# Delta rule: the eight z products of a slot that needs new weights, from rounds 0 and 6 to 12 to rounds 6 to 12

## The chip, the cores and the metric

The kernel runs on one core of one Trainium2 chip. The metric is the device time of one execution in microseconds, and a lower one is better. All data is float32.

## The reference, cut to what matters

The program computes two transformer blocks over 256 tokens and 256 context tokens. The change lies in the delta-rule mixer of the second block. Cut to that:

```
z = proj[..., DN_CONV_W:DN_CONV_W + DN_VAL_W]          # 512 rows of tokens x 2048
def step(S, inp):
    qc, kc, vc, gc, bc = inp
    a = eye + where(strict, kk * decay * bc, 0)
    sol = triangular_solve(a, rhs)
    u, w = sol[..., :dv], sol[..., dv:]
    v_new = u - w @ S
    o = (qc * exp(gc)) @ S + qk @ v_new
    S = S * exp(g_last) + (kc * exp(g_last - gc)).T @ v_new
    return S, o
...
o = rmsnorm_2(o_f + flip(o_b), norm_g) * silu(z)
return o @ w_out
```

So z is a plain matrix product (the layer's input by 2048 columns of `dn_w_in`) which nothing in the recurrence needs: it is wanted only after it. The recurrence is a chain. Each chunk needs the inverse of a triangular matrix, and each state needs the one before.

## The kernel before, in words

The kernel is written by hand for five engines. Each engine has a program of its own (`pe_program`, `dve_program` and so on), and each runs its instructions strictly in the order written. A wait for a semaphore therefore holds all that stands behind it on that engine.

The delta rule works in **slots**, k from 0 to 17 (`pe_chunks` and its likes). A slot has 13 **rounds**, 0 to 12. In each round every engine issues, one after the other, what several generators have for that round. On TensorE these are, in this order:

- `pe_inverse` of chunk group k: a chain of four levels, each of three steps. In rounds 0, 3, 6 and 9 it transposes W (L2135), in rounds 1, 4, 7 and 10 it multiplies by N (L2143), in rounds 2, 5, 8 and 11 by T (L2151). Between the three steps VectorE makes R (L2165), ScalarE makes T (L211), and VectorE updates W (L2169).
- `pe_prep` of the next group (L2007, L2008 and L2015).
- `pe_zstep`: one 128x512 tile of z, as eight products that add up in one PSUM bank (L2454). The table `Z` says how many of the eight are issued in which round. Sixteen tiles fill slots 0 to 15. The four slots of a column chunk c = k // 4 share one weight chunk of 2 MB; i = k % 4 is the row tile.
- `pe_recur` of group k - 2: for both directions the state's products (L2281 or L2288, L2297, L199, L2318). From round 1 on, VectorE answers with the carry (L2335, four instructions a direction), ScalarE with copies and scalings (L211), GpSimd with masks.

The weights of z come through a ring of four slots. Three of them are lent out to hold other data during the delta rule, so one slot is left. `ring.use` makes TensorE wait for the load (semaphore `ring3`), and `sp_zsteps` on SyncE issues the load of the next chunk (L183) only when the last product of the chunk before (`nz.p` of slot 4c - 1, round 12) is done. On SyncE the load stands behind the z store (L2490) and two small loads of decays for the queries (L1962), and ahead of two more (L1954). ScalarE copies the finished tile in round 12.

PSUM banks are handed out by `Banks.take` from a queue of idle ones: the one that was given back first is taken first, and TensorE waits for what has to have read it. The z tile holds its bank from its first product to the end of the slot.

Of the kernel before, what the change touches and what calls it, by code (L numbers as in the profile page):

```python
# [188 lines left out]
def bc(ap, axis, n):  # L189
    u = ap.unsqueeze(axis)  # L190
    shape = list(u.shape)
    shape[axis] = n
    return u.to_broadcast(shape)
# [70 lines left out]
class Kernel:  # L264
# [1734 lines left out]
    def pe_prep(self, p, m, k):  # L1999
        P, V = self.P, self.V  # L2000
        g, c = divmod(k, 4)
        for r in range(self.ROUNDS):
# [9 lines left out]
            if r == 8:  # L2012
                p.wait_ge(*V.of("in.Z", k))
                b = self.banks.take(p, "in.ab", k)
# [67 lines left out]
    def dve_block(self, v, m, k, part):  # L2082
# [10 lines left out]
        if part == 2:  # L2093
            for d in range(2):
                t = v().tensor_tensor(m["prod"][:, 256 * d:256 * d + 256].rearrange("p (h j r) -> p h j r", h=4, j=8),
                                      bc(m["AC"][:, d], 2, 8), bc(bc(m["start"][:, 4 * d, :], 1, 4), 3, 8), ALU.mult)
                t.then_inc(*(V.up("in.Z", k) if d else V.up("in.Z0")))

# [343 lines left out]

    Z = {0: 1, 6: 1, 8: 1, 9: 2, 10: 1, 11: 1, 12: 1}

    def pe_zstep(self, p, m, k):
        c, i = divmod(k, 4)
        if i == 0:
            m["zch"] = self.ring.use(p, 8, 512)  # L2450
        b, q = self.banks.take(p, "nz.p", k), 0
        for r in range(self.ROUNDS):
            for _ in range(self.Z.get(r, 0)):
                t = p.e.matmul(b, self.hT[:, q, 128 * i:128 * i + 128], m["zch"][:, q, :], start=(q == 0), stop=(q == 7))  # L2454
                if q == 7:
                    t.then_inc(*self.P.up("nz.p", k))
                q += 1
            yield
        self.banks.give(("nz.p", k), self.A.of("nz.z", k))
        if i == 3:  # L2460
            self.ring.done(self.P.of("nz.p", k))
            if c < 3:
                m["lent"] = [self.ring.lend() for _ in range(3)]
# [1555 lines left out]
```

## Time and profile before

| | us |
|---|---|
| median of 3 runs | 4279.09 |
| lowest and highest | 4276.19, 4282.1 |
| span of the profiled execution | 4275.4 |
| TensorE busy | 3506.1 (82%) |
| VectorE busy | 2659.6 (62%) |
| ScalarE busy | 1401.6 (33%) |
| GpSimd busy | 1205.5 (28%) |
| mean granted TensorE clock (1 is 2.4 GHz) | 0.947 |

The profile was taken from one execution. Of its own time only the span, from the first to the last instruction, is shown. It is 3.7 us below the median of the runs. Slots 0 to 15 of the delta rule lie between about 1262 and 1847 us of the span. The wait of an instruction is shown behind it in square brackets, with what ended it. A float32 matmul is recorded as two instructions, so one product of z is an entry "x2".

### The profile page before, as it was taken

What the parts mean: (1) busy time and instruction counts of PE and PEld (TensorE: products, weight loads), DVE (VectorE), ACT (ScalarE), POOL (GpSimd) and SP (SyncE); (2) the same over time, 40 slices, a digit from 0 to 9 for tenths busy, and PEclk for the clock granted to TensorE, in tenths of its full rate; (3) what the DMA queues carried; (4) which work ended last, traced back from release to release, by engine and by line L of the source; (5) the groups of instructions that cost most, each with busy time, mean ns of one, the idle gap of its engine ahead of it and who ended that gap; (6) DMA issues with size and microseconds to landing.
All of it is one profiled execution on the core that took longest, in us unless ns stands there. A gap on an engine that the chain in (4) does not pass through costs nothing.

```text
span 4275.4 us, 38801 instructions
## 1 busy us (share of the span) xinstructions
PE 3506.1 (82%) x11382; PEld 1852.2 (43%) x11382; DVE 2659.6 (62%) x5456; ACT 1401.6 (33%) x3747; POOL 1205.5 (28%) x1228
## 2 busy tenths in 40 slices
PE   7888978999867677779998987877788787877877
PEld 3334436844335555567554542322233256322222
DVE  3656455849656666633779658777555455887444
ACT  1232120004524544441333333433433221433333
POOL 0001100001005444520333433433434201434432
PEclk9889989999989998989999999999999998999999
DMA  5523324645321111043899999999999723999998
GB/s 215 197 79 136 121 85 165 224 165 189 138 71 33 52 52 57 17 166 143 349 415 397 406 409 421 403 422 421 409 417 413 326 79 142 413 421 414 417 421 360
DMA packets 169764, 1088.28 MB, mean 255 GB/s; under 512 B 16432, under 2 KB 45488, under 8 KB 51152
## 3 DMA queue, kind: packets, MB, share of 16 engines
q0 software_dynamic: 112608, 820.04, 46.7%
q1 hardware_dynamic: 56944, 265.77, 16.9%
q8 instruction: 90, 1.47, 0.1%
q14 instruction: 122, 1.00, 0.1%
HBM read 1075.19 MB, written 10.55 MB: 254 GB/s over the span
## 4 chain that ended last, share of the span: by engine, by line
PE 34%; DVE 24%; DMA 18%; issue 12%; POOL 7%; ACT 6%; DVEq 0%; SPq 0%; POOLq 0%; ACTq 0%
PE bank L199 19%; DMA arena<-in_uv,arena 15%; POOL arena L3018 6%; DVE arena L3035 6%; ACT arena L211 5%; PE bank L2986 4%; DVE arena L443 2%; PE bank L1620 2%; DVE arena L561 2%; PE bank L2454 2%; DVE arena L217 1%; PE bank L2151 1%; PE bank L2143 1%; DVE arena L221 1%; DMA arena<-in_w_rows 1%
## 5 line engine op out<-in xcount | busy, mean ns | idle before, releaser
L2986 PE MATMUL bank<-arena 128*128 128x512 f32 x3072 | 1486.8, 618 | 355.0 <-ACT arena L211 352.2
L211 ACT ACTIVATE arena<-arena 128x1 f32<-128x1 f32 (+4 forms) x2831 | 949.6, 335 | 2005.7 <-DVE arena L3035 1123.7
L199 PE MATMUL bank<-arena 128*128 128x256 f32 (+4 forms) x4640 | 1298.6, 439 | 69.8 <-ACT arena L211 35.3
L3035 DVE CUSTOM_DVE_ANT_0 arena<-arena 128x1024 f32<-128x1024 f32 x768 | 941.8, 1226 | 607.2 <-DMA arena<-in_uv,arena 568.9
L3018 POOL DMA_INDIRECT arena<-in_uv,arena x768 | 791.0, 1030 | 1254.2 <-PE bank L2986 856.7
L2986 PEld LDWEIGHTS bank<-arena 128*128 128x128 f32 x3072 | 544.5, 191 | 1269.9 <-ACT arena L211 825.4
L199 PEld LDWEIGHTS bank<-arena 128*128 128x128 f32 (+2 forms) x4640 | 805.1, 196 | 551.9 <-issue 424.2
L211 ACT ACTIVATE arena<-bank 128x512 f32<-128x512 f32 (+4 forms) x306 | 160.8, 525 | 496.5 <-PE bank L199 318.6
L443 DVE CUSTOM_DVE_ANT_0 arena<-arena 128x1024 f32<-128x1024 f32 x192 | 241.2, 1256 | 33.5 <-DMA arena<-in_w_rows 21.9
L211 ACT ACTIVATE arena<-bank,arena 128x128 f32<-128x128 f32 (+1 forms) x400 | 162.4, 406 | 286.8 <-PE bank L2143 224.2
L626 POOL TENSOR_SCALAR arena<-arena 128x1 f32<-128x1 f32 (+3 forms) x48 | 16.2, 337 | 665.2 <-ACT arena L211 471.0
L561 DVE SCALAR_TENSOR_TENSOR arena<-bank,arena 128x508 f32<-128x508 f32 (+2 forms) x248 | 159.0, 641 | 8.8
L2454 PE MATMUL bank<-arena 128*128 128x512 f32 x256 | 134.3, 628 | 30.3 <-DMA arena<-in_dn_w 30.3
L211 ACT ACT_TABLE_LOAD x92 | 118.0, 1283 | 79.4 <-DMA arena<-gates_rest 26.5
L217 DVE TENSOR_SCALAR arena<-bank,arena 128x256 f32<-128x256 f32 (+3 forms) x162 | 84.1, 519 | 88.4 <-PE bank L520 48.4
L2151 PE MATMUL bank<-arena 128*128 128x128 f32 x512 | 75.7, 292 | 60.5 <-ACT arena L211 60.5
L2201 POOL TENSOR_TENSOR arena<-arena 128x512 f32<-128x512 f32 x64 | 81.2, 1269 | 117.0 <-DVE arena L2169 70.0
L2194 POOL TENSOR_TENSOR arena<-arena 128x512 f32<-128x512 f32 x64 | 82.5, 1290 | 99.6 <-PE bank L2143 96.4
L216 DVE TENSOR_SCALAR arena<-bank,arena 128x256 f32<-128x256 f32 (+5 forms) x98 | 55.4, 565 | 80.6 <-PE bank L199 63.1
L2151 PEld LDWEIGHTS bank<-arena 128*128 128x128 f32 x512 | 63.2, 194 | 86.3 <-ACT arena L211 85.7
L2169 DVE TENSOR_TENSOR arena<-arena,bank 128x512 f32<-128x512 f32 x64 | 44.0, 687 | 75.9 <-PE bank L2151 73.5
L221 DVE TENSOR_REDUCE arena<-arena 128x32 f32<-128x512 f32 (+10 forms) x99 | 66.1, 668 | 39.9 <-ACT arena L211 34.4
(251 smaller groups left out, 2493.4 us busy)
## 6 DMA issues: line engine op xcount, KB each, us to landing
arena<-in_w_rows SPq DMA_DIRECT2D x50, 1024.0 KB, 5.0
arena<-in_w_in SPq DMA_DIRECT2D x16, 2048.0 KB, 8.0
arena<-in_wq SPq DMA_DIRECT2D x14, 2048.0 KB, 8.5
arena<-in_dn_w SPq DMA_DIRECT2D x12, 2048.0 KB, 10.0
arena<-in_w_up SPq DMA_DIRECT2D x11, 2048.0 KB, 7.9
arena<-in_dn_wo SPq DMA_DIRECT2D x8, 2048.0 KB, 11.3
arena<-in_w_rows POOLq DMA_DIRECT2D x14, 1024.0 KB, 5.7
arena<-decay_rest SPq DMA_DIRECT2D x56, 256.0 KB, 5.0
```

Source lines behind the costliest of these rows:

```text
L199: t = p.e.matmul(out, l, r, start=(i == 0), stop=(i == n - 1))
L211: return a().activation(out, in_, f, **kw)
L217: return v().tensor_scalar(out, a, s1, s2, op0, op1)
L221: return v().tensor_reduce(out, a, AX, op)
L443: v().tensor_tensor_reduce(trash, w[:, j, :], self.crow[r], 1.0, 0.0, ALU.mult, ALU.add, self.M[m][:, j0 + j, c:c + 1]).then_inc(*(V.up("m ...
L561: t = v().scalar_tensor_tensor(dst[:, :, o], src[:, :, f], wc(d + h), dst[:, :, o], ALU.mult, ALU.add)
L1620: t = p.e.matmul(bs[n], m["act"][:, 4 * c + k, 128 * i:128 * i + 128], ch[:, k, 512 * half:512 * half + 512], start=(c + k == 0), stop=(4 ...
L2151: t = p.e.matmul(b[:, H4[h]], m["T"][:, H4[h]], m["B"][:, H4[h]], start=True, stop=True)
L2454: t = p.e.matmul(b, self.hT[:, q, 128 * i:128 * i + 128], m["zch"][:, q, :], start=(q == 0), stop=(q == 7))
L2986: t = p.e.matmul(by[half], m["dg"][ee % 4], m["uv"][r][:, 1024 + 512 * half:1536 + 512 * half], start=(ee == 0), stop=(ee == 127))
L3018: g.e.indirect_dma_start(out=m["uv"][q % 7], out_offset=None, in_=self.I["uv"], in_offset=bass.IndirectOffsetOnAxis(ap=m["idx"][n % 2][:, ...
L3035: v().tensor_tensor_reduce(self.spare, uv[:, 0:1024], m["ht"][n % 2], 1.0, 0.0, ALU.mult, ALU.add, m["acts"][:, ee:ee + 1]).then_inc(*V.up ...
```

## The change

`Z` becomes two tables. A slot with i = 0 (slots 0, 4, 8 and 12, where a new weight chunk is needed) issues its eight products in rounds 6, 7, 8, 9 (two), 10, 11 and 12. The other slots keep round 0 and rounds 6, 8, 9 (two), 10, 11 and 12. `ring.use` and `banks.take` are called right ahead of the first product and no longer at the slot's start.

```
-    Z = {0: 1, 6: 1, 8: 1, 9: 2, 10: 1, 11: 1, 12: 1}
+    Z = ({6: 1, 7: 1, 8: 1, 9: 2, 10: 1, 11: 1, 12: 1}, {0: 1, 6: 1, 8: 1, 9: 2, 10: 1, 11: 1, 12: 1})
...
         c, i = divmod(k, 4)
-        if i == 0:
-            m["zch"] = self.ring.use(p, 8, 512)
-        b, q = self.banks.take(p, "nz.p", k), 0
+        q = 0
         for r in range(self.ROUNDS):
-            for _ in range(self.Z.get(r, 0)):
+            for _ in range(self.Z[min(i, 1)].get(r, 0)):
+                if q == 0:
+                    if i == 0:
+                        m["zch"] = self.ring.use(p, 8, 512)
+                    b = self.banks.take(p, "nz.p", k)
                 t = p.e.matmul(b, self.hT[:, q, 128 * i:128 * i + 128], m["zch"][:, q, :], start=(q == 0), stop=(q == 7))
```

The order of the other engines' and of SyncE's instructions stays. On TensorE, the start of slot 4 before (the last product of slot 3, the transposes of round 0, then the z product with the wait for the weights, then round 0 to 3 of the others):

```order
L2454 MATMUL bank<-arena 128x512 x2
L2135 MATMUL bank<-arena 128x128 x4
L2454 MATMUL bank<-arena 128x512
L2288 MATMUL bank<-arena 128x256 x2
L2143 MATMUL bank<-arena 128x128 x4
L2288 MATMUL bank<-arena 128x256 x2
L2151 MATMUL bank<-arena 128x128 x4
L2297 MATMUL bank<-arena 128x128 x4
L2135 MATMUL bank<-arena 128x128 x4
```

The same place in the changed program (lines below the diff are two higher, so z is L2456):

```order
L2456 MATMUL bank<-arena 128x512 x2
L2135 MATMUL bank<-arena 128x128 x4
L2288 MATMUL bank<-arena 128x256 x2
L2143 MATMUL bank<-arena 128x128 x4
L2288 MATMUL bank<-arena 128x256 x2
L2151 MATMUL bank<-arena 128x128 x4
L2297 MATMUL bank<-arena 128x128 x4
L2135 MATMUL bank<-arena 128x128 x4
```

The z product of round 0 is gone, and with it the wait that stood ahead of L2288, L2143 and all the rest of the slot.

On TensorE, rounds 6 to 8 of slot 4 before:

```order
L2135 MATMUL bank<-arena 128x128 x4
L2454 MATMUL bank<-arena 128x512
L2318 MATMUL bank<-arena 128x256 x2
L2143 MATMUL bank<-arena 128x128 x4
L2318 MATMUL bank<-arena 128x256 x2
L2151 MATMUL bank<-arena 128x128 x4
```

And in the changed program:

```order
L2135 MATMUL bank<-arena 128x128 x4
L2456 MATMUL bank<-arena 128x512
L2318 MATMUL bank<-arena 128x256 x2
L2143 MATMUL bank<-arena 128x128 x4
L2456 MATMUL bank<-arena 128x512
L2318 MATMUL bank<-arena 128x256 x2
L2151 MATMUL bank<-arena 128x128 x4
```

The product of round 6 is now the slot's first and carries the wait for the weights; a second one stands in round 7, between L2143 and the second L2318.

## Rows read from the trace of the kernel before

**Rows 1.** The page, part 1: busy time of each engine, share of the span.

```profile
PE 3506.1 (82%) x11382; PEld 1852.2 (43%) x11382; DVE 2659.6 (62%) x5456; ACT 1401.6 (33%) x3747; POOL 1205.5 (28%) x1228
```

**Rows 2.** Waits: who waited for whom, us in total, times, longest.

```profile
PE bank L2454 <- DMA arena<-in_dn_w: 30.3, 3, 10.3
```

**Rows 3.** Timeline of TensorE, slot 4 to round 3: start, us, instruction, idle before.

```profile
1396.62 0.66 PE L2135 MATMUL bank<-arena 128*128 128x128 f32 x4 [1.91 <-DVE arena L2121]
1407.56 2.08 PE L2454 MATMUL bank<-arena 128*128 128x512 f32 x2 [10.29 <-DMA arena<-in_dn_w]
1409.43 1.91 PE L2288 MATMUL bank<-arena 128*128 128x256 f32 x4
...
1416.95 0.66 PE L2135 MATMUL bank<-arena 128*128 128x128 f32 x4 [0.68 <-DVE arena L2169]
```

**Rows 4.** Busy time in stretches: PE, PEld, DVE, ACT, POOL, granted clock, DMA.

```profile
1396.00:1400.00 4.00, 0.66 (x4) 0.42 (x4) 1.25 (x2) 2.68 (x7) 2.54 (x3) 0.78 0.48 137
1400.00:1407.00 7.00, 0.00 (x0) 0.00 (x0) 0.00 (x0) 0.00 (x0) 0.00 (x0) 0.50 1.00 385
```

**Rows 5.** Timeline of TensorE, slot 5 from round 0 to round 3.

```profile
1443.10 0.66 PE L2135 MATMUL bank<-arena 128*128 128x128 f32 x4 [1.90 <-DVE arena L2121]
...
1444.46 1.03 PE L2288 MATMUL bank<-arena 128*128 128x256 f32 x4
1445.32 1.05 PE L2143 MATMUL bank<-arena 128*128 128x128 f32 x8
...
1448.03 1.16 PE L2151 MATMUL bank<-arena 128*128 128x128 f32 x8 [0.79 <-ACT arena L211]
...
1450.77 0.66 PE L2135 MATMUL bank<-arena 128*128 128x128 f32 x4 [0.68 <-DVE arena L2169]
```

**Rows 6.** Timeline of VectorE, slot 5, the same rounds.

```profile
1445.52 1.51 DVE L2335 SCALAR_TENSOR_TENSOR arena<-bank,arena 128x128 f32<-128x128 f32 x4 [1.03 <-PE bank L2288]
...
1448.41 1.51 DVE L2335 SCALAR_TENSOR_TENSOR arena<-bank,arena 128x128 f32<-128x128 f32 x4
1450.02 0.69 DVE L2169 TENSOR_TENSOR arena<-arena,bank 128x512 f32<-128x512 f32 x1
```

**Rows 7.** Timeline of TensorE, slot 5, rounds 6 and 7: a product that waits for R.

```profile
1459.85 0.60 PE L2135 MATMUL bank<-arena 128*128 128x128 f32 x4
...
1461.68 1.13 PE L2143 MATMUL bank<-arena 128*128 128x128 f32 x8 [0.37 <-DVE arena L2165]
```

**Rows 8.** Timeline of TensorE, round 0 and round 3 of slot 8, then of slot 12.

```profile
1546.02 0.66 PE L2135 MATMUL bank<-arena 128*128 128x128 f32 x4 [1.91 <-DVE arena L2121]
...
1565.69 0.66 PE L2135 MATMUL bank<-arena 128*128 128x128 f32 x4
...
1698.36 0.91 PE L2135 MATMUL bank<-arena 128*128 128x128 f32 x4 [1.91 <-DVE arena L2121]
...
1718.05 0.66 PE L2135 MATMUL bank<-arena 128*128 128x128 f32 x4 [0.68 <-DVE arena L2169]
```

**Rows 9.** Timeline of TensorE, slot 4, z of round 6 and L2151 of round 8.

```profile
1425.17 1.02 PE L2454 MATMUL bank<-arena 128*128 128x512 f32 x2
...
1430.75 1.16 PE L2151 MATMUL bank<-arena 128*128 128x128 f32 x8 [1.94 <-ACT arena L211]
```

**Rows 10.** Timeline of SyncE: the issue of slot 4's weights.

```profile
1396.83 0.50 SPq L183 DMA_DIRECT2D arena<-in_dn_w  x1
```

**Rows 11.** DMA issues from 1396.8 to 1397.5 us: KB, us to landing.

```profile
arena<-in_dn_w SPq DMA_DIRECT2D x1, 2048.0 KB, 10.7
```

**Rows 12.** Landing of the eight L183 loads issued from 1243 to 1886 us.

```profile
DMA to landing us min/median/max: 10.3/11.6/30.1
```

**Rows 13.** Landing of the two query decays (L1962) issued at 1395.7 and 1396.2.

```profile
DMA to landing us min/median/max: 6.0/6.2/6.3
```

**Rows 14.** Timeline of TensorE, round 0 and round 3 of slot 11.

```profile
1663.99 0.67 PE L2135 MATMUL bank<-arena 128*128 128x128 f32 x4 [2.07 <-DVE arena L2121]
...
1673.34 0.66 PE L2135 MATMUL bank<-arena 128*128 128x128 f32 x4 [0.68 <-DVE arena L2169]
```

## The prediction

> **What bounds the kernel now.** I read the busy shares first, then the waits, then the timelines of the engines around the slots that need new weights.
>
> TensorE is busy 82% of the span and no other engine over 62% [rows 1]. A share says little about one stage, so the question is what TensorE waits for in the delta rule. The list of waits has one row that the change can touch. The z product (L2454) waited three times for its weights, 30.3 us in all and 10.3 at most [rows 2]. It is three and not four because slot 0's weights are loaded long before; slots 4, 8 and 12 wait.
>
> The timeline shows what that wait holds up. In slot 4 TensorE issues the transposes of round 0 at 1396.62. The z product behind them starts at 1407.56, after 10.29 us of nothing [rows 3]. The load was issued at 1396.83 [rows 10] and took 10.7 us [rows 11], so it landed at 1407.5. During this, from 1400 to 1407, no engine does anything at all, and the clock of TensorE stands at 0.50, its 1.2 GHz level [rows 4]. The reader should see that everybody's next step needs a TensorE product that is queued behind z. The wait is thus bare in full. Its end is cold as well: L2288 takes 1.91 us behind it [rows 3] against 1.03 in slot 5 [rows 5].
>
> From the transposes of round 0 to those of round 3, a slot with this wait takes 1416.95 - 1396.62 = 20.33 us in slot 4 [rows 3], 19.67 in slot 8 and 19.69 in slot 12 [rows 8]. Slot 5 does the same work, its z product of round 0 included, in 1450.77 - 1443.10 = 7.67 us [rows 5].
>
> **The change, part by part.**
>
> *The wait leaves round 0.* Compared with slot 5, slots 4, 8 and 12 lose 12.66, 12.00 and 12.02 us: 36.7 in all. This is 30.3 of bare wait and 6.4 of cold clock behind it.
>
> *The z product leaves round 0.* In slot 5 L2288 starts 1.36 us after the transposes and L2143 2.22 after them [rows 5]. Between them and the transposes stands one z product, 0.86 from start to start, as from L2288 to L2143. Which chain does it lengthen? On VectorE the first carry starts at 1445.52, 1.06 after L2288; the second carry starts 2.89 later, takes 1.51 and is followed by the update of W at 1450.02 and by the transposes at 1450.77 [rows 5, 6]. Without z, this chain starts 0.86 earlier: round 3 would come 7.67 - 0.86 = 6.81 after round 0. The other chain goes through R. Where TensorE waits for R it starts L2143 1.83 after the transposes [rows 7], so L2143 moves from 2.22 to 1.83 and not by the full 0.86. L2151 follows 2.71 after L2143 and lasts 1.16 [rows 5]: it ends at 1.83 + 2.71 + 1.16 = 5.70. The second carry ends at (1448.41 - 1443.10) - 0.86 + 1.51 = 5.96. The carry is later, and its 6.81 stands. Bounds: 0 and 0.86 per slot; I take 0.86, since this chain ends last in the rows.
>
> So the three slots save 20.33 - 6.81 = 13.52, 19.67 - 6.81 = 12.86 and 19.69 - 6.81 = 12.88: 39.3 us. Slot 0 has no wait and no carry, only the R chain: I credit 0.4 (2.22 - 1.83), bounds 0 and 0.86.
>
> *A z product comes to round 7.* It stands between L2143 and the second L2318, and the next thing on TensorE, L2151, waits 1.94 us for ScalarE in slot 4 [rows 9]. The product needs 0.86 of that. The second L2318 comes 0.86 later, and VectorE's and ScalarE's answers to it are needed only in later rounds. Cost: nothing, as long as ScalarE ends last there. If that cover is gone, it is 0.86 in each of four slots, 3.4 us. I take 0.
>
> *The wait moves to round 6.* Behind it on TensorE would stand both L2318, L2143 of round 7 and all the rest, and every engine behind those. Is it still a wait? Before, z of round 6 started at 1425.17 [rows 9], 28.55 after the transposes of round 0. Shortened by 13.52 it comes at 15.03. The load is issued 0.21 after these transposes and takes 10.7 [rows 10, 11]: it lands at 10.9. The margin is 4.1 us in slot 4. So I take 0. The nearest row is that very load; the far bound is the longest landing among the eight big loads of this half, 30.1 us [rows 12], and it makes a rival.
>
> *SyncE and its queue.* The load's place in SyncE's order and its release (the last z product of the slot before) do not change, nor does any DMA. But what was hidden under the wait may now be late. The query decays issued ahead of the load land 6.0 to 6.3 us after their issue [rows 13], so by about 1402.5. ScalarE needs the first of them in round 2, whose L2151 would begin at 1396.62 + 1.83 + 2.71 = 1401.2, behind another exponential. So this is tight: between 0 and 1402.5 - 1401.2 = 1.3 a slot. I take 0, since that exponential waits for VectorE's work behind the first carry.
>
> *The bank.* The z tile takes its bank six rounds later. Banks are reused in the order in which they came back. So before round 6 one bank more is idle and every wait for a bank gets slack; from round 6 on the queue is as before. Cost 0.
>
> *The clock.* TensorE falls to 1.2 GHz at some slot starts even without a wait for weights. Slot 11 needs 1673.34 - 1663.99 = 9.35 us to round 3 [rows 14], 1.68 more than slot 5. I charge one of the three slots with that: -1.7 of gain. Bounds: none of them, or all three and slot 0 (6.7).
>
> **Sum:** 39.3 + 0.4 - 1.7 = 38.0 us. All of it is on the path, since all engines stand still in the wait and the stages behind the delta rule start on its last instruction. Against the profiled execution, 4275.4 - 38.0 = 4237.4 of span. The median of the runs is 3.7 above that span, so I forecast 4279.1 - 38.0 = **4241.1 us**.
>
> **The rivals.**
>
> *Cold starts.* With no product between the transposes and L2288, TensorE does less at the start of a slot, where it has just idled for 1.91 us. If that drops the clock in all four slots, the gain is 39.7 - 4 x 1.68 = 33.0, time 4246. For it: slot 11 fell with z in place. Against: slot 5 stayed at full speed after the same idle time, and 0.86 us of work is little. The Trainium skill ("TensorE: Matmul & The Clock Gate", "What's actually happening") says that the low clock is the default and that activity lifts it. By that rule the wait costs more than its length, as the trace shows with 0.50; but by the same rule a product used as filler at a sparse place is worth something, and the change takes it away. The sum by it would be this rival's.
>
> *Backlog.* The wait let the others catch up. From 1396 to 1400 ScalarE worked 2.68 us and GpSimd 2.54 [rows 4]. If this work now delays the slot, each gives back up to 2.7: gain 38.0 - 8.1 = 29.9, time 4249. Against: slot 5 starts with the same work on both and needs 7.67.
>
> *The load is late in round 6.* If it lands more than 4.1 us later because four engines now work beside it, each microsecond more costs one per slot. At 18 us instead of 10.7 it is 3 x 3.2 = 9.6 of wait: gain 28, time 4251, or less gain with a cold clock behind it. Against: the DMA traffic is the same as before.
>
> *Nothing arrives.* The time comes back at a later stage: 4279. I see no stage that starts on anything but the delta rule's end.
>
> *Slower: the load becomes as slow as the slowest of its kind.* At 30.1 us [rows 12] it lands 30.3 after the transposes. TensorE then waits 15.3 us in round 6, and z of round 6 comes at 30.3 instead of 28.55: 1.8 later than before. The clock is down again behind it, some 2.2 us (6.4 / 3). That is 4 per slot, 12 in all: 4291. It decides from a landing of about 26 us on. Against: the 30.1 belongs to a burst of several 2 MB loads; here there is one such load beside four small ones.
>
> **How the numbers follow.** Forecast 0.68, cold starts 0.12, backlog 0.08, late load 0.05, nothing 0.03, slower 0.04. About 0.2% (8.6 us) is what a measurement of this kernel can tell from no change. The first four cases are all faster than that: 0.93; same 0.03; slower 0.04. The range goes from 4234 (no clock charge, 39.7, and the runs' own spread of 3 us and a little more) to 4252 (backlog, or the late load).
>
> **What would show it.** Right: no wait for in_dn_w on L2456; the other engines busy between round 0 and round 3 of slots 4, 8 and 12; 6.8 us for that stretch; the idle time ahead of L2151 in round 8 down from 1.94 to about 1.1; the delta rule shorter by 38, everything behind it as long as before. Wrong: a wait for weights at round 6 (late load); more than 8 us for the stretch at full clock (backlog) or at 1.2 GHz (cold starts); an unchanged end with a new wait behind the delta rule.

## The result and the profile after

The changed kernel takes 4234.72 us (median of 4 runs, 4233.56 to 4238.67), the kernel before 4280.6 (4 runs, 4276.19 to 4282.99). The ratio is 0.9896, with a 95% interval from 0.9883 to 0.9909. The gain is 45.9 us, against 38.0 forecast; the time forecast was 4241.1, and 4234.72 lies only 0.7 us above the lower end of the stated range (4234 to 4252). Between the two profiled executions the span fell from 4275.4 to 4231.8, by 43.6.

Page, part 1, of the changed kernel: the instructions of each engine are as many as in [rows 1], and their busy times differ by 16 us at most, while the span is 43.6 shorter.

```profile
span 4231.8 us, 38794 instructions
PE 3498.2 (83%) x11382; PEld 1848.0 (44%) x11382; DVE 2659.4 (63%) x5456; ACT 1401.4 (33%) x3747; POOL 1221.3 (29%) x1228
```

What the z product (now L2456) waited for, and who waited for it, from the view of its line. The row of [rows 2] has no counterpart: nothing in this list is a DMA.

```profile
its engine sat idle before it (us, times) until:
  issue: 22.9, 94
who waited for it (us, times):
  ACT arena L211: 42.3, 16
```

Timeline of TensorE in slot 4, from round 0 to round 3 and then rounds 6 to 8. It answers to [rows 3, 9].

```profile
1397.58 0.66 PE L2135 MATMUL bank<-arena 128*128 128x128 f32 x4 [1.91 <-DVE arena L2121]
1398.07 1.03 PE L2288 MATMUL bank<-arena 128*128 128x256 f32 x4
1399.11 1.13 PE L2143 MATMUL bank<-arena 128*128 128x128 f32 x8
...
1404.74 0.66 PE L2135 MATMUL bank<-arena 128*128 128x128 f32 x4 [0.79 <-DVE arena L2169]
...
1412.95 1.02 PE L2456 MATMUL bank<-arena 128*128 128x512 f32 x2
...
1415.57 1.02 PE L2456 MATMUL bank<-arena 128*128 128x512 f32 x2
...
1418.53 1.16 PE L2151 MATMUL bank<-arena 128*128 128x128 f32 x8 [1.07 <-ACT arena L211]
1419.52 1.02 PE L2015 MATMUL bank<-arena 128*128 128x512 f32 x2
```

Round 0 to round 3 takes 1404.74 - 1397.58 = 7.16 us where it took 20.33. The first z product starts 15.37 us after the transposes, the second fills part of the idle time ahead of L2151, which is 1.07 in place of 1.94.

The load is issued at the same place, and the same stretches as in [rows 4] now hold work of every engine at full clock (columns: stretch, length, PE, PEld, DVE, ACT, POOL, granted clock, DMA share, GB/s). The weights still arrive after 10.7 us beside it (365 GB/s from 1400 to 1407, against 385).

```profile
1397.80 0.50 SPq L183 DMA_DIRECT2D arena<-in_dn_w  x1
```

```profile
arena<-in_dn_w SPq DMA_DIRECT2D x1, 2048.0 KB, 10.7
```

```profile
1396.00:1400.00 4.00, 2.41 (x16) 1.99 (x17) 2.87 (x9) 3.52 (x9) 2.36 (x4) 1.00 0.36 109
1400.00:1407.00 7.00, 5.42 (x43) 4.77 (x42) 5.63 (x10) 5.43 (x12) 3.65 (x4) 1.00 0.98 365
```

To see where the time went, I took the start of the round-0 transposes of every slot from the TensorE timelines of both kernels, and the first matmul behind the last z product of slot 15 (1847.51 and 1807.89) as the end.

| us | before | after | gain |
|---|---|---|---|
| start of slot 0 | 1268.28 | 1266.97 | 1.3 |
| slot 0 | 31.86 | 34.35 | -2.5 |
| slot 4 (to round 3) | 46.48 (20.33) | 33.29 (7.16) | 13.2 |
| slot 8 | 45.87 (19.67) | 33.34 (7.16) | 12.5 |
| slot 12 | 47.58 (19.69) | 33.86 (7.68) | 13.7 |
| the other twelve slots together | 407.44 | 406.08 | 1.4 |
| all of slots 0 to 15 | 579.23 | 540.92 | 38.3 |
| from there to the end of the span | 2427.9 | 2423.9 | 4.0 |

So the gain sits where it was looked for. Of the 39.4 us of slots 4, 8 and 12, 37.7 lie ahead of round 3. The other 1.7 lie in round 8 of slot 12: there the kernel before waited 1.99 us for ScalarE and ran at 1.2 GHz behind it.

```profile
1733.01 1.92 PE L2015 MATMUL bank<-arena 128*128 128x512 f32 x2
1734.71 1.75 PE L2454 MATMUL bank<-arena 128*128 128x512 f32 x2
```

Two lines of the table were not expected: slot 0 is slower, and 4 us come from behind the delta rule.

### The profile page after: what moved, and what is told of

It reads as the page before. It is cut to its first block, busy times and chain, and to the rows that moved or that the text cites. A ratio compares the mean times of both kernels' runs of the same rounds, so it can differ in the third digit from the quotient of the medians.

```text
span 4231.8 us, 38794 instructions
## 1 busy us (share of the span) xinstructions
PE 3498.2 (83%) x11382; PEld 1848.0 (44%) x11382; DVE 2659.4 (63%) x5456; ACT 1401.4 (33%) x3747; POOL 1221.3 (29%) x1228
## 3 DMA queue, kind: packets, MB, share of 16 engines
q8 instruction: 90, 1.47, 0.1%
## 4 chain that ended last, share of the span: by engine, by line
PE 34%; DVE 24%; DMA 19%; issue 11%; ACT 6%; POOL 6%; DVEq 0%; POOLq 0%; ACTq 0%; SPq 0%
PE bank L199 20%; DMA arena<-in_uv,arena 17%; DVE arena L3037 6%; ACT arena L211 6%; POOL arena L3020 5%; PE bank L2988 4%; DVE arena L443 2%; PE bank L1620 2%; DVE arena L561 2%; DVE arena L217 1%; PE bank L2456 1%; PE bank L2151 1%; PE bank L2143 1%; DVE arena L221 1%; DMA arena<-in_w_rows 1%
## 5 line engine op out<-in xcount | busy, mean ns | idle before, releaser
L3020 POOL DMA_INDIRECT arena<-in_uv,arena x768 | 805.0, 1048 | 1239.4 <-PE bank L2988 842.7
L211 ACT ACT_TABLE_LOAD x92 | 118.0, 1283 | 78.9 <-DMA arena<-gates_rest 26.2
L2456 PE MATMUL bank<-arena 128*128 128x512 f32 x256 | 130.7, 614 | 0.0
L2151 PE MATMUL bank<-arena 128*128 128x128 f32 x512 | 76.7, 294 | 56.9 <-ACT arena L211 56.9
L2151 PEld LDWEIGHTS bank<-arena 128*128 128x128 f32 x512 | 64.2, 197 | 83.5 <-ACT arena L211 82.9
L2194 POOL TENSOR_TENSOR arena<-arena 128x512 f32<-128x512 f32 x64 | 83.1, 1298 | 60.7 <-PE bank L2143 57.1
```

Source lines behind the costliest of these rows:

```text
L211: return a().activation(out, in_, f, **kw)
L2151: t = p.e.matmul(b[:, H4[h]], m["T"][:, H4[h]], m["B"][:, H4[h]], start=True, stop=True)
L3020: g.e.indirect_dma_start(out=m["uv"][q % 7], out_offset=None, in_=self.I["uv"], in_offset=bass.IndirectOffsetOnAxis(ap=m["idx"][n % 2][:, ...
```

## The experiments

**The changed kernel again, beside the next three.**

> The changed kernel once more, on the same chip as the next three. Wait theory (the wait for weights left round 0 and nothing took its place): slots 4, 8 and 12 take 7.2 to 7.7 us from round 0 to round 3, slots 0 to 15 about 541 us, the time 38 to 46 us below the kernel before. The 4 us that the changed kernel gained behind the delta rule are either chance in TensorE's clock (then they vary: 0 to 6 us here) or belong to the change (then again about 4).

It took 4237.57 us (4234.88 to 4240.89) against 4282.23; ratio 0.9900 (0.9884 to 0.9917). Slots 4, 8 and 12 took 7.16, 7.16 and 7.65 to round 3, all sixteen slots 541.46. From the end of slot 15 to the first gather of the experts (L3020) it took 156.1 us; the kernel before had taken 156.6 there and the first profile of the changed one 152.8. So the 4 us did not come back, and are not the change's.

**The kernel before, profiled again.**

> The kernel before, profiled a second time. If the 2.5 us that slot 0 lost and the 4 us gained behind the delta rule are chance in TensorE's clock, slot 0 takes 34 to 35 us here and the stretch from the end of slot 15 to the first gather about 153 us; if they belong to the change, 31.9 and 156.6 us again. Slots 4, 8 and 12: waits of 10 us each again.

It took 4280.77 us in its one run. Slot 0 took 33.52, which neither case of the expectation names. The stretch to the first gather took 155.7, nearer to the first profile's 156.6 than to the 153 expected of chance: by itself this run doesn't settle the 4 us, the changed kernel's 156.1 does. All sixteen slots took 588.8 us, 9.6 more than in the first profile of the same kernel, though the three waits are the same:

```profile
PE bank L2454 <- DMA arena<-in_dn_w: 30.1, 3, 10.3
```

What is longer are slots 0, 1, 7, 8 and 13, by 1.7, 3.6, 1.7, 1.8 and 1.4 us; slot 14 is 0.6 shorter, and the others agree within 0.2. The mean granted clock of the sixteen slots is 0.91, against 0.93 in the first profile. Round 8 of slot 8, from the TensorE timeline and the windows around it (columns as above), shows what happens in one of them. TensorE waits 2.00 us for ScalarE, and behind that wait it runs at 1.2 GHz for a while: the z product takes 1.91 in place of 1.02.

```profile
1581.89 1.16 PE L2151 MATMUL bank<-arena 128*128 128x128 f32 x8 [2.00 <-ACT arena L211]
1582.89 1.58 PE L2015 MATMUL bank<-arena 128*128 128x512 f32 x2
1584.26 1.91 PE L2454 MATMUL bank<-arena 128*128 128x512 f32 x2
```

```profile
1580.00:1582.00 2.00, 0.10 (x1) 0.11 (x1) 1.78 (x3) 1.72 (x6) 0.38 (x1) 1.00 0.00 0
1582.00:1586.00 4.00, 4.00 (x13) 2.02 (x14) 0.69 (x1) 1.55 (x8) 2.00 (x2) 0.65 0.01 2
```

So the first profile of the kernel before, on which the forecast rests, had met fewer such places. Of the 9.6 us only 3.6 show in the span (4279.0 against 4275.4): slot 0 began 4.8 us earlier here, and the part behind slot 15 was 1.1 shorter.

**Slot 0 as before.**

```
-            for _ in range(self.Z[min(i, 1)].get(r, 0)):
+            for _ in range(self.Z[min(i, 1) if k else 1].get(r, 0)):
```

> Slot 0 issues its z products in rounds 0 and 6 to 12 again; slots 4, 8 and 12 stay as changed. Clock theory for slot 0 (the product in round 0 is what lifts TensorE to 2.4 GHz early there): slot 0 takes 31.9 us again in place of 34.3, the time is 2.5 us below the changed kernel's. Rival (chance): slot 0 takes 33 to 35 us here too, no difference.

The time was 4240.13 us (4230.66 to 4242.16), ratio 0.9899 (0.9882 to 0.9915), no different from the changed kernel. Slot 0 took 35.06 us with its product back in round 0. The clock theory for slot 0 falls. With the product in round 0 TensorE did reach its high clock sooner (7.73 us to round 3, against 8.55 in the changed kernel), but from round 3 to round 6 the granted clock was 0.50 again and the slot was no shorter. The 31.86 of the first profile did not come back in the four other profiles with the product in round 0 (33.52 to 35.06): it was luck.

**The old order without the wait.** Z's weights are loaded once, and slots 4, 8 and 12 use them again, so there is nothing to wait for and z stays in round 0. Three quarters of z are then computed with the wrong weights; the work is the same.

```
     def pe_zstep(self, p, m, k):
...
         if i == 0:
-            m["zch"] = self.ring.use(p, 8, 512)
+            if c == 0:
+                m["zch"] = self.ring.use(p, 8, 512)
+            else:
+                self.ring.lend()
...
     def sp_zsteps(self, s, m):
...
-                self.ring.load(s, self.I["dn_w"][8 + c], 8, 512)
+                if c == 0:
+                    self.ring.load(s, self.I["dn_w"][8 + c], 8, 512)
+                else:
+                    self.ring.skip()
```

> The order of the kernel before (z in round 0 everywhere), but the z weights of chunks 1 to 3 are not loaded: chunk 0's serve for all, so three quarters of z are other numbers. Takes away the wait without moving a product. Wait theory: round 0 to round 3 of slots 4, 8 and 12 takes 7.7 us as in slot 5, the delta rule is 36 to 39 us shorter than before, the changed kernel is at most 2 us faster than this. Rival (the order matters by itself): this gains 30 us or less.

It took 4248.36 us (4239.74 to 4254.19), ratio 0.9923 (0.9904 to 0.9942). Round 0 to round 3 took 7.66 and 7.65 in slots 4 and 8, as predicted from slot 5, and 9.34 in slot 12, with a cold start. But the three slots took 35.51, 35.54 and 35.53 us, 1.7 to 2.2 more than in the changed kernel, and the sixteen slots 550.76. Removing the wait alone seems to give less than the change: 10.8 us less between the medians (4237.57 for the changed kernel beside it), though the intervals of the two ratios overlap a little, and 9.3 less over the sixteen slots of one profile each. Slot 4 shows why, again in round 8 (z is L2457 here):

```profile
1419.58 1.25 PE L2151 MATMUL bank<-arena 128*128 128x128 f32 x8 [1.94 <-ACT arena L211]
1420.62 1.92 PE L2015 MATMUL bank<-arena 128*128 128x512 f32 x2
1422.33 1.82 PE L2457 MATMUL bank<-arena 128*128 128x512 f32 x2
```

```profile
1418.00:1420.00 2.00, 0.42 (x3) 0.43 (x4) 1.51 (x3) 1.81 (x6) 0.12 (x1) 1.00 0.00 0
1420.00:1424.00 4.00, 4.00 (x12) 1.88 (x11) 0.69 (x1) 1.23 (x7) 2.22 (x2) 0.57 0.01 2
```

In the changed kernel the same instructions take 1.16, 1.02 and 1.02 and the clock there is 1.00 (from 1419 to 1423). The moved product sits in this very wait. That gave a new theory: **the product in round 7 is filler that keeps the clock up.** Filler is work that nobody waits for, put where the engine would idle. Two runs test it.

**The product of round 7 to round 12**, in the changed kernel:

```
-    Z = ({6: 1, 7: 1, 8: 1, 9: 2, 10: 1, 11: 1, 12: 1}, ...
+    Z = ({6: 1, 8: 1, 9: 2, 10: 1, 11: 1, 12: 2}, ...
```

> In slots 0, 4, 8 and 12 the product of round 7 stands in round 12 (two there); all else as changed. Filler theory (the product in round 7 fills the wait ahead of L2151 of round 8 and so keeps TensorE at 2.4 GHz): with that wait back at 1.9 us, slots 4, 8 and 12 take 27.8 us from round 3 to their end in place of 26.1, 1.7 each, as in the run without loads; 5 us in all. Rival (it is only issue order, the clock is chance): 26.1 us there, no difference.

It took 4240.36 us (4239.03 to 4249.67), ratio 0.9921 (0.9904 to 0.9937), an interval that overlaps the changed kernel's. The wait ahead of L2151 was back at 1.94 to 1.99 us in all three slots. Slot 4 fell to the low clock behind it and took 27.8 us from round 3 to its end; slots 8 and 12 did not and took 26.2. One of three, where the expectation said all three: the wait alone doesn't decide it, and neither the theory's case (all three) nor the rival's (none) came true.

```profile
1417.18 1.16 PE L2151 MATMUL bank<-arena 128*128 128x128 f32 x8 [1.94 <-ACT arena L211]
1418.18 1.65 PE L2015 MATMUL bank<-arena 128*128 128x512 f32 x2
1419.62 1.91 PE L2456 MATMUL bank<-arena 128*128 128x512 f32 x2
```

**The product of round 8 to round 7**, in the old order without loads:

```
+    Z7 = {0: 1, 6: 1, 7: 1, 9: 2, 10: 1, 11: 1, 12: 1}
...
-            for _ in range(self.Z.get(r, 0)):
+            for _ in range((self.Z if i else self.Z7).get(r, 0)):
```

> The order of the kernel before without the later loads (three quarters of z are other numbers), and in slots 0, 4, 8 and 12 the product of round 8 stands in round 7. Filler theory: the wait ahead of L2151 of round 8 falls from 1.94 to 1.07 us and TensorE stays at 2.4 GHz: slots 4, 8 and 12 take 26.1 us from round 3 to their end, where the same kernel without this move took 27.9 in all three. Rival (chance): 27.9 in at least one of them.

(The expectation has it wrong that all three slots had taken 27.9 without this move: it was 27.8 and 27.9 in slots 4 and 8, and 26.2 in slot 12, whose loss lay at its start.) The time was 4237.67 us in its one run. Slots 4, 8 and 12 took 25.45, 25.50 and 25.49 us from round 3 to their end, with no low clock in round 8. It is 0.6 less than the 26.1 expected, since one product less stands in round 8.

```profile
1418.17 1.16 PE L2151 MATMUL bank<-arena 128*128 128x128 f32 x8 [1.07 <-ACT arena L211]
1419.17 1.02 PE L2015 MATMUL bank<-arena 128*128 128x512 f32 x2
1420.11 0.66 PE L2135 MATMUL bank<-arena 128*128 128x128 f32 x4
```

All profiles together are clearer. I took the time from the transposes of round 6 to those of round 9 in slots 4, 8 and 12. Without a product in round 7 (both profiles of the kernel before, the old order without loads, and the product moved to round 12) it was 10.15 to 10.47 us in 6 of 12 cases, and 8.73 to 8.79 in the other 6. With the product in round 7 (eight profiles of seven kernels; the quarters below, whose load comes late, are left out) it was long in none of 24. So the product is worth 1.7 us in about every second such slot; my estimate is 2.5 us in all on average, and a rough one, since the cases are few and several stand in one profile.

Slots 5, 9 and 13 bear this out. They need no new weights, and their wait ahead of the same L2151 is 1.66 us. Without a product in round 7 the stretch from round 6 to round 9 was long there (8.80 to 9.00 in place of 7.33) in 8 of 33 cases, in slot 13 of the changed kernel both times. In the two kernels that put a product there (the next two runs) the wait was 0.80 and the stretch long in none of 6.

**All slots late.**

```
-            for _ in range(self.Z[min(i, 1)].get(r, 0)):
+            for _ in range(self.Z[0].get(r, 0)):
```

> All sixteen slots issue z in rounds 6 to 12. Carry theory (the product in round 0 lengthens VectorE's chain of carries): round 0 to round 3 falls from 7.66 to 7.16 us in slots 3, 5, 7, 9, 11, 13 and 15, 3.5 us in all, and nothing in the slots without carries; round 7 costs 0.1 us in some. Time 3 us below the changed kernel's. Filler rival: slot starts without the product fall to 1.2 GHz more often, 1 to 1.7 us each; time 3 to 10 us above the changed kernel's.

It took 4235.53 us (4229.68 to 4239.6), ratio 0.9888 (0.9872 to 0.9905): not to be told from the changed kernel. The trace tells more. In slots 3, 5, 7, 9 and 13 the stretch to round 3 fell from 7.66 to 7.22 or 7.23, the carry's part. In slots 11 and 15, which start at the low clock in the changed kernel, it fell from 9.35 to 8.46 and from 8.56 to 6.26. Against that, slot 1 took 33.71 in place of 30.32 and slot 14 9.27 to round 3 in place of 7.98, both at the low clock. The sixteen slots took 539.5. Both theories were partly right and nearly cancel.

**Late only where there are carries.**

```
-            for _ in range(self.Z[min(i, 1)].get(r, 0)):
+            for _ in range(self.Z[0 if i == 0 or (i != 2 and k > 2) else 1].get(r, 0)):
```

> As changed, and the slots with carries (3, 5, 7, 9, 11, 13 and 15) issue z in rounds 6 to 12 too; slots 1, 2, 6, 10 and 14 keep round 0. Carry theory: seven slots shorter by 0.4 us each in the stretch from round 0 to round 3, delta rule 538 us in place of 541; time 3 us below the changed kernel's, which the clock's chance can hide. Filler rival: their starts fall to 1.2 GHz more often, no gain or a loss.

The sixteen slots took 536.7 us, the least of all profiles, and the time was 4230.92 us (4229.23 to 4241.14), ratio 0.9888 (0.9872 to 0.9905). The seven stretches took 7.22 to 7.44. The direction is as expected, but 536.7 is one profile, and the ratio's interval overlaps that of the changed kernel (0.9884 to 0.9917 in its second measurement), so that this version beats it is not shown.

**How much margin does the load have?** Three runs. First the changed kernel with one load of z's weights (`ring.load` for c = 0 alone, as above).

> The changed order, the z weights of chunks 1 to 3 not loaded (chunk 0's serve for all, three quarters of z are other numbers). Hidden theory (the load costs nothing where it now lies): slots as in the changed kernel within 0.3 us, delta rule 541 us. Rival (the load still slows ScalarE or the decays beside it): slots 4, 8 and 12 shorter by over 0.3 us each.

It took 4236.65 us (4234.67 to 4239.4), ratio 0.9904 (0.9888 to 0.9921). Slots 4, 8 and 12 took 33.30, 33.34 and 33.65, the sixteen slots 541.91. The loads that the changed kernel makes cost it nothing measurable. From the old order without loads it differs in the order alone. That one had ratio 0.9923 beside another measurement of the kernel before; the intervals overlap, so the medians show this difference less surely than the slots do: 4, 8 and 12 took 106.6 us there and 100.3 here.

Then the loads made late, in halves and in quarters. SyncE waits for each part before it issues the next, which also holds the two decay loads behind it (in quarters, to 1411.49 in slot 4):

```
+        for j in range(n):
+            lo, hi = j * kt * w // n, (j + 1) * kt * w // n
+            if j:
+                s.wait_ge(self.sems[i], self.count[i])
+            self.count[i] += 16
+            s.e.dma_start(self.aps[i][:, lo:hi], src[:, lo:hi]).then_inc(self.sems[i], 16)
```

> Each later z chunk is loaded in two halves, the second issued when the first has landed. Margin theory (4 us left at round 6): landing about 14 us after round 0 in place of 11, round 6 comes at 15: no wait or less than 1 us, delta rule 541 to 544 us. Rival (the margin is smaller than the rows say): waits of 2 us or more.

No wait, slots of 33.30, 33.33 and 33.82 us, 4237.78 us in its one run. The two halves of slot 4 took 7.0 us each from issue to landing.

> The same in four quarters, each about 5.5 us: landing 21 to 23 us after round 0. Margin theory: the first z product waits 6 to 8 us in each of slots 4, 8 and 12, and TensorE is at 1.2 GHz behind it: 8 to 10 us a slot, 24 to 30 in all, about 4263 us. This is the point from which the moved wait costs as the old one did.

It took 4245.17 us (4243.71 to 4250.03), ratio 0.9928 (0.9912 to 0.9945). The view of in_dn_w has 9.1 us of wait in three times, and the timeline of slot 4 shows the wait in its new place, with the low clock behind it. The last two lines are the same place in slot 12, where the clock stayed up:

```profile
  PE bank L2460: 9.1, 3
```

```profile
1397.05 0.66 PE L2139 MATMUL bank<-arena 128*128 128x128 f32 x4 [1.91 <-DVE arena L2125]
...
1415.56 1.97 PE L2460 MATMUL bank<-arena 128*128 128x512 f32 x2 [2.98 <-DMA arena<-in_dn_w]
1417.33 1.91 PE L2322 MATMUL bank<-arena 128*128 128x256 f32 x4
...
1696.95 1.13 PE L2460 MATMUL bank<-arena 128*128 128x512 f32 x2 [3.01 <-DMA arena<-in_dn_w]
1697.91 1.03 PE L2322 MATMUL bank<-arena 128*128 128x256 f32 x4
```

The weights were there 1415.56 - 1397.05 = 18.5 us after the transposes, and z began 3.1 us later than in the changed kernel. Slots 4 and 8 grew by 3.80 and 3.89 us: these 3.1, and some 1.8 of cold clock (z and the L2322 behind it took 1.77 and 1.70 from start to start, against 0.86 each), less the 1.1 that TensorE had idled ahead of L2151 of round 8 and no longer did (a wait of 0.00 there). In slot 12 the clock stayed up, and from round 3 to its end it grew by 2.09 only; the whole slot grew by 1.58, since its start was at full clock this time. The parts were quicker than expected (4.2 us each, not 5.5), so the wait was 3 and not 6 to 8, but the margin is as reckoned: two halves one after the other are free, and weights that are there at 18.5 us are three late.

## Why the prediction was right, point by point

- *The wait of 30.3 us is bare and goes.* Right. The wait is gone, nothing took its place, the old order without loads shows that its removal alone brings most of the gain, and new_once (the changed kernel with one load) shows that the load beside the work costs nothing.
- *The stretch from round 0 to round 3 falls to 6.81 us.* It was 7.16 in slots 4 and 8. The first carry did start 0.86 earlier (1.56 us after the transposes, against 2.42 in slot 5 before). But VectorE's L2051 between the two carries took 1.47 us, against 1.11 in slot 5 before (between the two carries of [rows 6]). The changed kernel's slot 4, on VectorE and on GpSimd:

```profile
1399.14 1.51 DVE L2335 SCALAR_TENSOR_TENSOR arena<-bank,arena 128x128 f32<-128x128 f32 x4 [0.17 <-PE bank L2288]
1400.78 1.47 DVE L2051 TENSOR_TENSOR arena<-arena 128x512 f32<-128x512 f32 x1
1402.38 1.51 DVE L2335 SCALAR_TENSOR_TENSOR arena<-bank,arena 128x128 f32<-128x128 f32 x4
```

```profile
1400.44 1.26 POOL L2194 TENSOR_TENSOR arena<-arena 128x512 f32<-128x512 f32 x1
```

  The same two in slot 5 of the kernel before:

```profile
1447.17 1.11 DVE L2051 TENSOR_TENSOR arena<-arena 128x512 f32<-128x512 f32 x1
```

```profile
1446.46 1.26 POOL L2194 TENSOR_TENSOR arena<-arena 128x512 f32<-128x512 f32 x1 [0.59 <-PE bank L2143]
```

  In slot 5 they overlapped for 0.55 us, here for 0.92. What is left after L2194's end is the same in both, 1.11 - 0.55 = 0.56 and 1.47 - 0.92 = 0.55: L2051 does its work only when L2194 has finished. In every profile, wherever L2051 started while L2194 ran, it took 1.10 to 1.71 us, and 0.54 to 0.56 of it came after L2194's end. The Trainium skill ("SBUF — State Buffer", "SBUF: two separate sides") says that an operation of VectorE with two SBUF inputs and one of GpSimd that reads SBUF exclude each other, and these rows agree. The step of the sum that was off is thus that the whole chain moves by 0.86: L2051, longer by 0.36, took part of it back. No run removed L2194 or moved it, so this cause is read from rows and not tested. The z product cost 0.5 and not 0.86 in round 0, which all_late confirms (0.43 in five slots).
- *Slot 0, +0.4.* Not delivered. Without the product in round 0 its stretch to round 3 took 8.54 or 8.55 us in eight profiles, with it 7.73 to 9.05 in five; the whole slot took 33.4 to 34.8 without and 31.9 to 35.1 with. No gain shows.
- *The product in round 7 costs nothing.* It cost nothing, but the term was mis-sized: by the estimate above it is a gain of 2.5 us on average (1.7 us, three slots, 6 cases of 12), since it fills an idle time behind which TensorE's clock fell in 6 of 12 cases and with it in none of 24. The cover I named (1.94 us of waiting) had a price that I did not see. The rule of the Trainium skill that the prediction weighed ("TensorE: Matmul & The Clock Gate", "What's actually happening": the low clock is the default, activity lifts it) agrees with these rows. In slots 4, 8 and 12 its effect was at the product's new place and not, as my rival had it, at the old one.
- *No wait at round 6, margin 4.1 us.* Right. No wait in the changed kernel, none with halves, 3 us with quarters. The price that the rival of the late load put on each further microsecond, one per slot, leaves out the idle time ahead of L2151, which takes the first 1.1 back, and the clock, which added 1.8 in two of three slots.
- *Query decays and bank, 0.* Right as far as the stretch shows: 7.16 us leaves no room for a further wait beside L2051's 0.36.
- *Clock, -1.7.* One of the three starts, slot 12's, was cold as charged (L2288 took 1.92 us), but it cost 0.5 (7.68 against 7.16) and not 1.68, and it did so in both profiles.
- *Nothing comes back behind the delta rule.* Right. The 4.0 us gained there in the first pair of profiles are chance: over twelve other profiles the stretch to the first gather takes between 152.4 and 157.4 us.
- *The sum.* 38.0 against 45.9 between the medians. The sixteen slots gave 38.3 in the first pair of profiles, and that this is so near 38.0 is partly luck. Slots 4, 8 and 12 gave 37.7 ahead of round 3, where 39.3 - 1.7 = 37.6 was forecast: the clock charge was 1.2 too large, but L2051 made each of the three slots 0.36 longer than reckoned. Beside that stand 1.7 in round 8 of slot 12, -2.5 in slot 0 and 1.4 in slots for which the sum has no term. Of the 7.9 us that the medians gave beyond the forecast, 1.5 come from the kernel before, whose median was 4279.09 in the three runs that the forecast used and 4280.6 in four. About 2.5 is the estimate for the product in round 7. The rest stays open. Set against the second profile of the kernel before (588.8) the sixteen slots gave 47.9, so the base that the forecast's rows came from, one profile with few falls of the clock, may have made the sum too small. But in the twelve slots other than 0, 4, 8 and 12, where no product moved, the four profiles without the product in round 7 took 407.4 to 413.5 us and the seven with it 406.1 to 409.5. Whether that is chance or the new order's doing no run shows.
- *The rivals.* Cold starts: in slot 12, at 0.5 us, and none in slots 4 and 8; slot 0 was cold with and without its product. In all_late it did come true elsewhere, in slots 1 and 14. Backlog: no, since round 3 came after 7.16 us, below slot 5's 7.67. Late load: no. Nothing arrives: no. Slower: quarters shows the mechanism, with the weights 18.5 us after the transposes in place of 10.9.

## What to carry to other kernels

A wait on an in-order engine costs what stands behind it, so look for the latest place at which its consumer can stand: here, six rounds later, it had 4 us to spare. Work that nobody waits for is best placed ahead of an instruction that waits anyway. There its own 0.86 us cost nothing here, and on TensorE it kept the clock up as well, worth about as much again on average (2.5 us over three slots). And take two profiles of the kernel before as the base of a sum, if its engine's clock comes and goes.

## What the runs showed of the hardware

- In round 8 of slots 4, 8 and 12 an idle time of 1.94 to 2.00 us of TensorE was followed by the 1.2 GHz level in 6 of 12 cases, one of 1.07 to 1.14 us in none of 24. In slots 5, 9 and 13 one of 1.66 us was followed by it in 8 of 33, one of 0.80 in none of 6. Behind it the slot took 1.7 us longer. A wait of 2.98 to 3.12 us in round 6 was followed by it in two cases of three.
- VectorE's L2051 (two SBUF inputs) took 1.10 to 1.71 us where it started while GpSimd's L2194 ran, always 0.54 to 0.56 of it behind L2194's end.
- The same kernel's delta rule took 579.2 us in one execution and 588.8 in another, with the same waits for DMA (30.3 and 30.1). The mean granted clock was 0.93 and 0.91. The difference of 9.6 us is as large as what the new order gained over the old one without the wait (9.3).
- A 2 MB load beside four busy engines landed after 10.7 us in slot 4, as it had while all of them stood still; in slot 8 after 10.3 in both kernels, in slot 12 after 11.7 against 10.7.
